# Latent tiles one by one beside the experts, with longer distances between an attention unit's steps

## What is computed

```python
for i in range(DEPTH):                     # 2 layers
    mx = modulation(c, w_mod[i], b_mod[i]); mc = modulation(c_ctx, w_mod[i], b_mod[i])
    hx = modulate(rmsnorm(x, norm1[i]), mx[0], mx[1]); hc = ...
    ox, oc = mix_even(hx, hc, ...) if i % 2 == 0 else mix_odd(hx, hc, ...)
    x = x + mx[2] * ox
    hx = modulate(rmsnorm(x, norm2[i]), mx[3], mx[4])
    x = x + mx[5] * peer(hx, p_wq[i], p_keys[i], p_u[i], p_v[i])
    ...                                    # the same for the context h in layer 0

def mix_even(...):                         # 4 differential heads (A), 8 windowed heads with sinks (B)
    w = softmax(q1 k1) - lam * softmax(q2 k2)      # A: every latent token sees all 768
    ...                                    # B: context and a window of 128, plus a sink
    return concat(rmsnorm(oa, a_gn) * (1 - lam_init), ob) @ w_out

def peer(h, wq, sub_keys, u_tab, v_tab):
    q = (h @ wq).reshape(T, 8, 2, 128)
    s = einsum("thpd,hpnd->thpn", q, sub_keys)     # 16 score vectors of 128 a token
    # top 16 of each half, top 16 of their 256 sums: 8 x 16 = 128 experts a token
    a = gelu(einsum("tkd,td->tk", u_tab[eidx], h)) * gate
    return einsum("tk,tkd->td", a, v_tab[eidx])
```

## Time and profile before

| | us |
|---|---|
| median of the runs (3) | 5179.86 |
| lowest, highest | 5177.51, 5180.51 |
| time of the profiled execution | 5194.1 |
| span of its trace | 5192.9 |
| busy PE, DVE, ACT, POOL | 4052.6, 2664.8, 1681.4, 1832.9 |

### The profile page before, as it was taken

The page is one execution under the profiler, slowest core; times in us unless marked ns, Lnnn a source line. Parts: engine busy times, 40 slices in busy tenths (PEclk is TensorE's granted clock), DMA queues, the critical chain, the costliest instruction groups (busy, mean ns, idle before and its releaser), DMA issues. The chain is left out here.

```text
span 5192.9 us, 42388 instructions
## 1 busy us (share of the span) xinstructions
PE 4052.6 (78%) x11522; PEld 1879.0 (36%) x11522; DVE 2664.8 (51%) x5781; ACT 1681.4 (32%) x4833; POOL 1832.9 (35%) x1362
## 2 busy tenths in 40 slices
PE   6987757789867889977777787478559877777777
PEld 1442523345423445522222233255245422222222
DVE  1432276555576555576654411534354666566544
ACT  0112134434344433333333311340213333333333
POOL 0000022234332234355567500100013465665675
PEclk9998878899998899999999988785779999999999
DMA  7124367799987799999999920000259999999998
GB/s 273 37 74 156 121 259 260 270 394 400 421 337 267 279 364 405 421 421 420 420 412 422 377 83 14 4 2 1 80 211 415 408 421 421 421 420 415 421 420 364
DMA packets 268976, 1522.76 MB, mean 293 GB/s; under 512 B 31696, under 2 KB 51824, under 8 KB 103632
## 3 DMA queue, kind: packets, MB, share of 16 engines
q0 software_dynamic: 184704, 1342.31, 63.8%
q1 hardware_dynamic: 82112, 174.45, 9.4%
q10 hardware_dynamic: 1936, 3.48, 0.2%
HBM read 1509.55 MB, written 10.58 MB: 293 GB/s over the span
## 5 line engine op out<-in xcount | busy, mean ns | idle before, releaser
L2285 PE MATMUL ps<-ex_ring,ex_diag 128*128 128x512 f32 x5120 | 2588.7, 636 | 745.3 <-ACT ex_diag L2274 722.5
L2155 POOL DMA_INDIRECT ex_ring<-in_p_uv,ex_expert x1280 | 1771.3, 1384 | 2073.0 <-PE ps L2285 1471.0
L2248 DVE SCALAR_TENSOR_TENSOR ex_ring<-ex_ring,H 128x1024 f32<-128x1024 f32 x1280 | 1555.4, 1225 | 1043.4 <-DMA ex_ring<-in_p_uv,ex_expert 1025.2
L2285 PEld LDWEIGHTS ps<-ex_ring,ex_diag 128*128 128x128 f32 x5120 | 932.7, 197 | 2203.8 <-ACT ex_diag L2274 1417.0
L2268 ACT ACTIVATE ex_act_w<-ex_dots 128x1 f32<-128x1 f32 x1280 | 260.4, 203 | 1693.3 <-DVE ex_ring L2248 1679.7
L2274 ACT ACTIVATE ex_diag<-ident_sb,ex_weight 128x128 f32<-128x128 f32 x1280 | 516.4, 403 | 93.6 <-issue 4.1
L2270 ACT ACTIVATE ex_weight<-ex_act_w,ex_gates 128x1 f32<-128x1 f32 x1280 | 380.6, 297 | 90.3 <-issue 2.8
L445 POOL TENSOR_TENSOR R<-R,pout_tmp 128x512 f32<-128x512 f32 x12 | 15.2, 1264 | 523.2 <-DVEq L436 523.2
L876 PE MATMUL ps<-win_w,hT 128*128 128x512 f32 (+1 forms) x480 | 188.7, 555 | 2.4 <-PEq L270 1.4
L402 PE MATMUL ps<-win_w,hT 128*128 128x496 f32 x384 | 162.9, 586 | 2.9 <-PEq L270 1.7
L876 PEld LDWEIGHTS ps<-win_w,hT 128*128 128x128 f32 x480 | 91.6, 192 | 99.5 <-issue 97.1
(11 more groups left out here) (323 smaller groups left out, 3268.7 us busy)
## 6 DMA issues: line engine op xcount, KB each, us to landing
mod_w<-in_w_mod SPq DMA_DIRECT2D x12, 2048.0 KB
ca_mod_w<-in_w_mod SPq DMA_DIRECT2D x12, 2048.0 KB
bs_w<-in_p_wqk SPq DMA_DIRECT2D x38, 576.0 KB, 8.7
ex_ring<-in_p_uv,ex_expert POOLq DMA_INDIRECT x1280
pre_w<-in_p_wqk SPq DMA_DIRECT2D x32, 576.0 KB, 4.6
win_w<-in_e_w_in SPq DMA_DIRECT2D x9, 1024.0 KB, 8.3
bs_w<-in_e_w_out_tiles SPq DMA_DIRECT2D x16, 512.0 KB
ex_sc<-key_scores SPq DMA_DIRECT2D x32, 256.0 KB, 7.5
```

What stands on the lines that cost most here:

```text
L2155: pool.indirect_dma_start(ring[:, r, :], None, uv_rows, bass.IndirectOffsetOnAxis(ap=expert[:, t % 2, n:n + 1], axis=0),).then_inc(landed[ ...
L2248: dve.scalar_tensor_tensor(out=ring[:, r, 0:D], in0=ring[:, r, 0:D], scalar=1.0, in1=h_of(t + t0), op0=ALU.mult, op1=ALU.mult, accum_out=d ...
L2285: mm = pe.matmul(mix_banks(t)[:, half, :], diag[:, b, :], ring[:, r, D + half * BANK:D + (half + 1) * BANK], start=(n == 0), stop=(n == SL ...
```

## The change

- *Head units.* The steps move apart: find at b+3, exp at b+4, mix at b+7, and then rounds of at most four 128x128 blocks, three slots a round: turn at t, copy and value at t+2; take comes three slots after the last value. t is b+8 for A and b+6 for B. Scores fill 3 banks (or 1, for context) instead of 4, turned blocks have one bank and the output another; the middle bank is shared by the two softmaxes of a unit, so that PE waits on a semaphore (`split`) of its own between them. Probabilities and output have one copy; exp waits until the unit before has been turned.
- *Latent tiles one by one.* Tile x goes through attention, group norm, projection, second norm and late scores alone. The first tile's units are 9 slots apart, the other 24 units 15, from slot 73. The later steps of tile x stand at 79 + 120x and after it, its late scores from 44 slots on, 4.4 slots apart; attention of the next tiles runs on beside them. Output and query weights are loaded four times instead of twice, matmuls have 128 columns instead of 256. Everything after attention uses bank 7: query and score of a half head take it in turn, all eight query matmuls stand in one slot, and the next query waits for the copy of the last score. The three weight buffers are real ones.
- *The second norm's scale* `(1 + scale) * gain` is stored once by the norm of the context tiles and loaded for each tile, in place of two loads and one operation a group.
- *Context attention.* Two streams of units, one for each tile, 12 slots a unit, six slots shifted; a chunk of modulation every 8 of 102 slots (before: every 5 of 69).
- *Modulation weights.* The host lays w_mod out by chunks, so that a load has 16 KB in one run for each partition instead of eight runs of 2 KB. SP's loop in `start` is written out.
- *Layer 2's late scores* keep their banks; copy of the query stands at slot + 5 (before + 4), copy of the score at + 7 (before + 6), store at + 8.

```diff
-            self.at["find"].put(b + 1, n)
-            self.at["exp"].put(b + 2, n)
-            self.first_part.append(parts)
-            if i < A_HEADS:
-                self.at["mix"].put(b + 3, n)
+            self.at["find"].put(b + 3, n)
+            self.at["exp"].put(b + 4, n)
+            if a_head:
+                self.at["mix"].put(b + 7, n)
                 mixes += 1
-                for name, d in (("turn", 4), ("copy", 5), ("value", 6)):
-                    self.at[name].put(b + d, (n, 0))
-                parts += 1
-                end = b + 7
-            else:
-                for c in range(2):
-                    for name, d in (("turn", 3), ("copy", 4), ("value", 5)):
-                        self.at[name].put(b + d + 2 * c, (n, c))
-                parts += 2
-                end = b + 8
             self.mixes.append(mixes)
-            self.at["take"].put(end, n)
-            self.end.append(end)
-        self.parts = parts
-        self.first_part.append(parts)
+            self.first_round.append(len(self.rounds))
+            at = b + (8 if a_head else 6)
+            for first in range(0, len(parts), 4):
+                r = len(self.rounds)
+                self.rounds.append((n, parts[first:first + 4]))
+                for name, d in (("turn", 0), ("copy", 2), ("value", 2)):
+                    self.at[name].put(at + d, r)
+                at += 3
+            self.at["take"].put(at + 2, n)
+            self.end.append(at + 2)
+        self.first_round.append(len(self.rounds))
...
+            for c, col, kt, cnt, first, last in self.score_order(n):
+                rows_ = slice(c * A_DQK, (c + 1) * A_DQK)
+                if last:
+                    self.splits += 1
+                    pe.wait_ge(self.split, self.splits)
+                mm = pe.matmul(self.S[:, c, col:col + cnt * P], q_of(m, t)[rows_, i * P:(i + 1) * P],
+                               KV[rows_, kt:kt + cnt, keys], start=True, stop=True)
+                if first:
+                    mm.then_inc(self.split, 1)
...
+        for r in self.at["copy"](slot):
+            wide = len(self.rounds[r][1]) * P
+            act.wait_ge(self.turned, r + 1)
+            if r >= 2:
+                act.wait_ge(self.valued, r - 1)
+            act.copy(self.probsT[:, r % 2, 0:wide], self.T[:, 0:wide]).then_inc(self.copied, 1)
         for n in self.at["exp"](slot):
             t, i = self.units[n]
-            b, w = n % 2, len(self.blocks(n)) * P
+            w = len(self.blocks(n)) * P
             act.wait_ge(self.biased, n + 1)
+            if n:
+                act.wait_ge(self.turned, self.first_round[n])
...
-    units = [(t, i) for i in range(2 * A_HEADS) for t in range(CT)]
-    with Stage(nc, "ca") as s:
-        probs, probsT = s.sb("probs", [P, 2, 2, CT * P]), s.sb("probsT", [P, 2, CT * P])
-        heads = HeadUnits(m, s, units, [4 * n for n in range(len(units))], probs, probsT)
-        mods = NextModulation(nc, m, a, s)
-        slots = heads.end[-1] + 1
-        step = slots // mods.CH
+    with Stage(nc, "ca") as s, Stage(nc, "ca0") as s0, Stage(nc, "ca1") as s1:
+        mods = Modulation(m, a, s, 1, list(range(6 * D // BANK)))
+        heads = []
+        for t, st in enumerate((s0, s1)):
+            heads.append(HeadUnits(m, st, [(t, i) for i in range(2 * A_HEADS)], [12 * n + 6 * t for n in range(2 * A_HEADS)],
+                                   st.sb("probs", [P, 2, CT * P]), st.sb("probsT", [P, 2, BANK]), CT * P, 2 + t, 1, 4 + 2 * t, 5 + 2 * t))
+        slots = heads[1].end[-1] + 1
+        step = slots // len(mods.chunks)
...
+                per = KC if self.shared else 2
+                took = KC // per - 1
+                for k in range(0, KC, per):
+                    self.at["query"].put(slot + k // per, (u, k, per))
+                scored = slot + took + 2
+                self.add_item(scored, last_use)
+                self.at["query_copy"].put(slot + took + 2, u)
+                self.at["score"].put(scored, u)
+                self.at["score_copy"].put(slot + took + 4, u)
+                self.at["store"].put(slot + took + 5, u)
+                self.copied[u] = slot + took + 4
...
+                if self.shared and u:
+                    pe.wait_ge(self.late_ready, u)
...
+    POST, PITCH, N2, LATE = 79, 120, 32, 44
...
+        units = [(CT + x, i) for x in range(XT) for i in range(2 * A_HEADS)]
+        begin = [9 * k for k in range(2 * A_HEADS)] + [73 + 15 * k for k in range((XT - 1) * 2 * A_HEADS)]
+        self.heads = HeadUnits(m, s, units, begin, s.sb("probs", [P, 2, NT * P]), s.sb("probsT", [P, 2, BANK]), NT * P, 2, 3, 5, 6)
         out_slots, late_begin = [], []
...
+        for x in range(XT):
+            b = self.POST + self.PITCH * x
+            assert self.heads.end[8 * x + 7] < b
+            at = lambda name, d, item: self.at[name].put(b + d, item)
+            at("gn_root", 0, x)
+            at("gn_scale", 3, x)
+            for r in range(2):
+                at("o_turn", 4 + 3 * r, (x, r))
+                at("o_copy", 6 + 3 * r, (x, r))
+            at("g1_load", 0, x)
+            at("x_load", 8, x)
+            at("n2_load", self.N2 - 1, x)
+            out_slots.append([b + 10 + 11 * (c // 4) + 5 * (c % 4) // 2 for c in range(KC)])
+            for c in range(KC):
+                self.at["out"].put(out_slots[-1][c], (x, c))
+            for r in range(2):
+                self.at["out_take"].put(out_slots[-1][4 * r + 3] + 3, (x, r))
+                at("h_turn", self.N2 + 6 + 3 * r, (x, r))
+                at("h_copy", self.N2 + 8 + 3 * r, (x, r))
+            at("n2_square", self.N2, x)
+            at("n2_scale", self.N2 + 4, x)
+            at("n2_shift", self.N2 + 5, x)
+            late_begin.append(b + self.LATE)
+        self.late_at = {slot: x for x, slot in enumerate(late_begin)}
+        self.late = LateScores(m, a, s, 0, [[CT + x] for x in range(XT)], KC, out_slots, late_begin, [4.4] * XT,
+                               lambda tiles, k: self.hT[:, k, :], [7], [7])
...
+        for x in self.at["g1_load"](slot):
+            if x:
+                sp.wait_ge(self.h_ready, x)
+            sp.dma_start(self.scale[:, :], rows(self.m.mods[0, 0:1, 2 * D:3 * D])).then_inc(self.scale_loaded, 16)
+        for x in self.at["n2_load"](slot):
+            sp.wait_ge(self.out_taken, 2 * x + 2)
+            sp.dma_start(self.scale[:, :], rows(self.m.n2_scale)).then_inc(self.scale_loaded, 16)
+        for x in self.at["x_load"](slot):
+            sp.wait_ge(self.o_turned, 2 * x + 2)
+            sp.dma_start(self.m.R[:, CT + x, :], self.a["x"][0, x * P:(x + 1) * P, :]).then_inc(self.x_loaded, 16)
...
+                if keep is not None:
+                    sp.wait_ge(scaled, 1)
+                    sp.dma_start(keep, scale[0:1, 0, :]).then_inc(kept, 16)
+                    sp.wait_ge(kept, 16)
...
+    inputs["w_mod"] = inputs["w_mod"].reshape(L, P, KC, 6 * D // BANK, BANK).transpose(0, 3, 1, 2, 4)\
+        .reshape(L, 6 * D // BANK, P, KC * BANK)
```

522 lines of the change are left out of this document (212 added, 310 removed).

## The result

The changed kernel takes 4998.51 us (median of four runs, 4996.51 to 5001.69), the kernel before, run beside it, 5180.18 us: a ratio of 0.9646, with a 95% interval of 0.9633 to 0.9658. The gain is 182 us at the median and 194 us between the two profiled executions (spans 5192.9 and 4998.6 us, times 5194.1 and 5000.31). The forecast was 4994 us.

What follows compares the result with a forecast made beforehand. The prediction took coupling of in-order engines in the expert stage's attention stretches as the bound. Gains of 167 (expert stage), 7 (start) and 12 (context attention) sum to 186 us, so 5180 - 186 = 4994 us; range 4943 to 5090.

Steps and rivals of the forecast that it cites:

- The bound and its cause: First expert stage: in-order engines coupled by PE-to-DVE hand-overs one slot apart; 3.77 us a slot against a 2.50 us floor.
- The attention units: First expert stage: price beyond the floor falls from 7.7 to 1.0 us a unit, 32 us remain, 214 gained.
- The late scores and the projection: First expert stage: 27.3 MB more weight loads cost 65 us, from 97 to 162; about 2.87 us a slot.
- The tail: First expert stage: the choice's last 18 steps spread over at least 38 slots; 21 us become about 3, gain 18.
- The start: First modulation stage: weights in 16 KB runs shorten the wait for chunk one and a gap; 7 us gained, bounds 0 and 10.
- Context attention: Stage with modulation weights: two interleaved streams replace one; 12 us gained, bounds +10 (slower) and -25.
- The second term: Context attention: last chunk stands before two unit chains, so the tail falls from 15 us to about 8.
- The total: Whole kernel: 167 + 7 + 12 = 186 us gained, giving a median of 4994 us.
- The signs: Expert stage: 400 GB/s or more, VectorE waiting for gathers, clock near 1, about 2125 us, 64 key and 32 output loads.
- Rival 1: Expert-stage attention: half the coupling stays because probabilities and output have one copy; 93 us above forecast, 5087 us, chance 0.18.
- Rival 2: Late scores: query and score sharing one PSUM bank make PE wait for ScalarE; slower, about 5215 us, chance 0.05.
- Rival 3: Expert stage: nothing is moved where the time is, gathers late for their own reason; about 5175 us, chance 0.02.

Runs made afterwards that it cites:

- The square above: Expert-stage lengths, units dense by two tiles against sparse tile by tile: short distances 2290.1 (kernel before) and 2210.7 us; long distances 2198.6 and 2100.6 us (changed kernel).
- the half loads: Changed kernel with each of the 64 key and query weight loads of the first expert stage cut to its second half: 4952.97 us (one run).

## Why the prediction was right, and where it was not

*The bound and its cause: right.* The stage was held by the coupling of in-order engines. The square above shows that the room at a hand-over was needed, and that tiles one by one with sparser units gave as much again. The prediction named the hand-over from PE to DVE at the scores; the runs add that the values' hand-over to `take` had a price of its own (37 of 110 us), which the waits of the kernel before did not show among their largest rows. The prediction has VectorE one or two slots ahead of PE. By the records of both engines, the median lead is 0.75 slots where nothing runs beside the experts and 1.0 to 1.4 in the attention stretches of before, with up to four there; in the first 96 slots of the changed kernel it is 2.0.

*The attention units: right in kind, mis-sized.* The sum gave a unit 1.0 us, 32 in all. The stage is 2100.6 - 1920 = 181 us over the floor. At the measured 2.43 us for a MB, the 54.5 MB of weights (64 x 576 and 32 x 512 KB) are 132 of these. At the 416 GB/s of the 2100 us stretch the stage moves 873.6 MB, 68.3 beyond the 805.3 of 768 gathers; the 13.8 MB that are not these weights are 33 us more at 421 GB/s. 16 us are left for 32 units, the tail and the choice, so a unit costs at most 0.5 us (an estimate). The stage is 24 us shorter than the forecast's 2125 (22 by the gain, as the stage before has 2290 us when it is measured in this way, not 2292), and at least 16 of them are this term: the value was taken between bounds of 0 and 7.7, and the lower one was nearly right. The rest lies in the small terms, which no run separates.

*The late scores and the projection: right.* 65 us for 27.3 MB more is 2.38 us a MB, and the half loads give 2.43. The forecast of 2.87 us a slot is what the long stretch shows, though there the units are in it as well, which points once more to the units.

*The tail: right in direction, not shown by itself.* No stretch is left with the 3.14 us a slot and the DMA share of 0.95 of the earlier trace rows. Where the first latent tile's choice ends, its large operations still fall into slots 228 to 240, and the stretch around them stays at the limit of the transfers:

```profile
1230.00:1350.00 120.00, 105.40 (x382) 56.94 (x382) 100.78 (x219) 59.99 (x166) 49.32 (x41) 0.94 1.02 419
```

The last tile's choice lies in the stretch with 2.50 us a slot and costs nothing that can be seen. No run took the choice's steps by themselves.

*The start: right.* 7 us were forecast, 8.8 came, and putting the old layout back costs 7.6 us of time. The Trainium skill, DMA: Bandwidth & Descriptors, Specifications, has 512 B as the smallest run at line rate; by it nothing would have been gained. The stretches above don't agree fully: 382 GB/s at a DMA share of 1.04 with runs of 2 KB, 410 at 0.99 with 16 KB. Beside the rate stands the issue that is held up, on which that rule is silent; what share of the 8.8 us is which stays open.

*Context attention: this step failed.* The forecast was 12 us gained and 3.6 were lost. The prediction's own sign of a wrong forecast, "a context attention longer than before", thus came true. Two terms were wrong. The first was put at nothing: the prediction counted the same matmuls at the same price, though the change says that the middle bank is shared and that PE waits at `split`. Two matmuls that had run at the same time now run in turn, and the scores keep PE busy 23.5 us instead of 12.3. The run with two banks for one stream turned 4.8 us of this into 4.1 us of time, so the 11.2 us are most of the 15.6 by which the step was wrong. The second term is the tail, counted as some 7 us gained beside 5 of waits. The end behind the last chunk did fall from 14.8 to 8.4 us (kernel before, then changed):

```profile
484.10:499.00 14.90, 10.91 (x49) 7.35 (x48) 4.82 (x20) 4.92 (x18) 0.00 (x0) 0.64 0.00 0
```

```profile
485.60:494.00 8.40, 6.02 (x29) 4.41 (x28) 2.74 (x10) 2.56 (x8) 0.00 (x0) 0.75 0.00 0
```

But 4.9 of these 6.5 us are matmuls that now stand earlier in the stage, where they take time as well. PE's idle time behind the first load, the tail included, fell from 17.8 to 12.4 us, and its busy time rose by 10.0, of which the scores are 11.2. So the two streams gave 5.4 + 1.2 = 6.6 us and the first load 1.1, where 12 were forecast, and the scores took 11.2. The bounds (+10 to -25) held the result, but not for this reason.

*The total.* 4994 was forecast and 4998.5 measured, but not because each term was that near: the stage came out 22 us better (189.5 for 167), the start 2 better, context attention 16 worse. The remaining 12 us lie between the profiled executions and the medians: the spans differ by 194, the medians by 182, since the kernel before's profiled execution was 14 us over its median and the changed kernel's 2. The prediction carried its 186 from span to median without allowing for that. That the sum of these is 4 us is luck.

*The signs.* The rate, the waits for gathers and the loads came as forecast. The granted clock did not quite: 0.93 and 0.97 in the stretches with attention, where it was to be near 1.

*The rivals.* Rival 1 (half the coupling stays, for want of buffers) asked for ACT waiting for turns at some 3 us a unit: it waits 51.9 us in 32 units, 1.6 each, while the DMA share is 1.01, so little hangs on it. The Trainium skill, Perfetto Trace Analysis, Optimization Strategy, says that a repeating gap can be a sign of too few buffers; here one copy of everything with more distance and sparser units did better than two copies with less of both (2100.6 against 2198.6 us), so the repeating waits of the earlier trace rows went without another buffer. No run changes the number of buffers alone. Rival 2 (the shared bank of the late scores) would show as PE waiting for ScalarE at the late queries: no such wait stands in the trace of the stage. A shared bank did cost, but in the other stage and at the scores. Rival 3 (nothing moved where the time is) fell with the first number.

## What to carry to other kernels

Where in-order engines share slots with a stream that must be fed in time, find which engine leads, and put more than one slot between a step of the engine behind and the step of the leading one that takes its result (three here); then spread the side work over the whole stage. Both were worth about the same here, and the second buffers that the kernel before had made neither unnecessary. Check what a change does to concurrency inside one engine as well: matmuls counted at the same number and the same duration can still cost twice the time when they lose the second bank. A shorter tail is a gain only as far as its waits go: work that moves to an earlier place still has to be done. A forecast that comes out right to 0.1% should still be checked term by term; here errors of 22 us one way and of 16 and 12 the other covered each other.

## What was not expected of the hardware

- Two 64-row matmuls of 256 columns to different banks take 0.70 us for four records, to one bank with a wait between them 1.45 us.
- The issue of a bias load on SP takes up to 13.96 us behind weight loads in runs of 2 KB, and 0.3 to 0.4 us behind runs of 16 KB, while the rate between 20 and 60 us differs only as 382 to 410 GB/s.
- The gathers of 8 KB rows beside plain loads hold 416 GB/s over 2100 us and 421 in single slices, at a DMA share of 1.01, and with a ring of 8 buffers this goes on while VectorE waits for gathers 311 times in 1400 us: those waits cost nothing.
